# A first stage rearranged: modulation rows on four 32-column tiles, step products inside hT's blocks, constant products in waits

## The chip, the cores and the metric

One program on one core of a Trainium2 chip. The number is the device time in microseconds of one execution, and the median of several. TensorE has a granted clock with two levels here, shown as 1.00 (2.4 GHz) and 0.50 (1.2 GHz).

## What is computed

Two transformer-like blocks on 512 tokens of width 1024, all in fp32; the change touches only the first steps of the first block:

```
mod   = silu(c)     @ w_mod + b_mod              # 6 parts: sh1, sc1, g1, sh2, sc2, g2
mod_c = silu(c_ctx) @ w_mod[:, :2D] + b_mod[:2D] # sh1_c, sc1_c
hc = rmsnorm(ctx, norm1_w) * (1 + sc1_c) + sh1_c # 256 context rows
h  = rmsnorm(x, norm1_w)   * (1 + sc1) + sh1     # 512 rows
dt = softplus(h @ w_in[:, OFF_DT:OFF_CF] + dt_bias)   # 64 columns, for both h and hc
```

Behind them come the projections, the scans, a mixture of experts and a second block, which are as before.

## The kernel before

The program writes each engine's queue by hand; `Steps` objects are semaphores with named steps, where `done` marks one and `after` waits for one. Six weight buffers `slot` of 2 MB stand in SBUF, and PSUM is the tensor `ps` of eight banks of 512 columns.

The first stage is everything ahead of the loop `pe.Fori(0, GROUPS)`, whose first products are those of line 1820.

- SP loads `w_mod` in four chunks of 2 MB into slots 0 to 3, with `xcT` (x and context, transposed, 3 MB) between the second and third (lines 1213, 1214). When the rows of the last chunk are done it goes on to the loop's weights. ScalarE's queue issues `prm`, `cst` and `w_dt` (lines 1358 to 1360).
- ScalarE computes `silu_c` (both conditioning vectors, 8 blocks of 2 columns), then the squares of `xcT` for the norm (`norm1.on_act`, line 445) and the roots (448).
- TensorE waits for `silu_c` and `cst`, makes the modulation rows of chunks 0 and 1 (line 1770: weights `silu_c[:, k, :]` of two columns, moving 512 columns of the chunk, eight k for each chunk, into two partitions of PSUM), then the sums of squares with the `ones` matrix (line 431), then chunks 2 and 3. An fp32 matrix product is two records in the trace; a transpose is one.
- VectorE takes the reciprocals of the roots (465), copies the rows out of PSUM (2375), and TensorE turns them into columns with 16 transposes (1774). VectorE adds the bias, makes `mod_scale` (2378 to 2384), and scales `hT` block by block (471); ScalarE adds the shift to each block (454).
- TensorE multiplies `hT` by `w_dt` (line 1786: six groups of 128 tokens, eight k for each, weights 128x128 of `hT`, moving 64 columns of `w_dt`). The outer loop is over token groups, so only the first group's products can follow the blocks as they come.
- Then `softplus` on VectorE and ScalarE (2391 to 2397, 1372 to 1376), three small cumulative products (1791, 1795, 1797) with their exponentials (1378 to 1382), and the loop begins.

Of the kernel before, what the change touches and what calls it, by code (L numbers as in the profile page):

```python
# [10 lines left out]
ACT = mybir.ActivationFunctionType  # L11
# [3 lines left out]
P = 128  # L15
D = 1024
KD = D // P
SEQ = 512
# [3 lines left out]
ALLT = TT + CT  # L22
# [30 lines left out]
PAIR_TABLE = UNITS // 2 + 3  # L53
# [66 lines left out]
class Columns:  # L120
# [8 lines left out]
    def __getitem__(self, name):  # L129
        a, n = self.at[name]  # L130
        return slice(a, a + n)


CST = Columns([("ident", P), ("ones", P), ("le", P), ("gt", P), ("ge", P), ("lt", P),
               ("expert", NE), ("odd", NE), ("unit", TABLE), ("filled", SEQ // UNIT), ("eps", 1), ("one", 1),
               ("spot", P), ("pair", PAIR_TABLE + 1), ("token", SEQ // P)])
PRM = Columns([("c", 2 * KD), ("b_mod", 2 * N_MOD * KD), ("norm1", KD), ("norm2", KD), ("final", KD),
               ("conv", GROUPS * 8 * (CONV_K + 1)), ("ssd_norm", 2 * KD),
               ("dt_bias", 2 * N_HEADS), ("a_log", 2 * N_HEADS), ("d_skip", N_HEADS), ("b_router", NE),
# [4 lines left out]
def program(nc, io):  # L144
# [22 lines left out]
    area = Area(FREE)  # L167
    slot = [area(f"slot{i}", [P, CHUNK]) for i in range(6)]
    SLOT_BYTES = CHUNK * 4
    cst = area("cst", [P, CST.width])  # L170
    prm = area("prm", [P, PRM.width])
# [3 lines left out]
    ps = nc.alloc_psum_tensor("ps", [P, 8, 512], F32)  # L175

    ident = cst[:, CST["ident"]]
# [3 lines left out]
    def sem(name):  # L181
        return nc.alloc_semaphore(name)
# [349 lines left out]
    area = Area(STAGE)  # L532
    hT = area("hT", [P, KD, W1])
# [1 line left out]
    mod_scale = area("mod_scale", [P, KD, 2])  # L535
    AFTER_H = area.next
    xcT = area("xcT", [P, KD, W1])
    silu_c = area("silu_c", [P, KD, 2])
    square = [area(f"square{i}", [P, W1]) for i in range(2)]
    root = area("root", [P, W1])  # L540
    mod_row = area("mod_row", [2, 2 * D // 512, 512])
    w_dt = area("w_dt", [P, KD, 2 * N_HEADS])

    s_cst = sem("s_cst")
    s_prm = sem("s_prm")
    s_x = sem("s_x")
    c_silu = Steps(sem("c_silu"), ["silu"])


    MOD_CHUNKS = 2 * D // 512  # L550
    MOD_FIRST = 2 * KD
    mods_pe = Steps(sem("mods_pe"), [f"rows{c}" for c in range(MOD_CHUNKS)] + ["turned"])
    mods_dve = Steps(sem("mods_dve"), ["rows", "bias"])
    for c in range(MOD_CHUNKS):
        loads[c] += 16

# [1 line left out]
    norm1 = Norm("norm1", KD, X_PARTS, lambda i: xcT[:, i, :], lambda i: hT[:, i, :],  # L558
                 lambda i, p: mod_scale[:, i, p:p + 1], lambda i, p: mod[:, i, p:p + 1],
                 square, root, 4, 1.0 / D)  # L560
# [5 lines left out]
    area = Area(AFTER_H)  # L566
    small = area("small", [P, 5, ALLT, 2 * N_HEADS])
    AFTER_SMALL = area.next
    area = Area(AFTER_SMALL)
# [7 lines left out]
    dt_psum = ps[:, 0, 0:ALLT * 64].rearrange("p (t h) -> p t h", h=64)  # L577
# [12 lines left out]
    area = Area(FREE + 2 * SLOT_BYTES, FREE + 6 * SLOT_BYTES)  # L590
# [9 lines left out]
    area = Area(AFTER_SMALL)  # L600
# [63 lines left out]
    area = Area(AFTER_Y)  # L664
# [6 lines left out]
    area = Area(AFTER_Y)  # L671
# [3 lines left out]
    area = Area(AFTER_F)  # L675
    c_row = area("c_row", [P, D])
    dft_seq = area("dft_seq", [P, 2 * SEQ])
    area = Area(AFTER_F)
    gate_sT = [area(f"gate_sT{i}", [P, 2, SEQ]) for i in range(2)]
    area = Area(FREE + SLOT_BYTES, FREE + 2 * SLOT_BYTES)  # L680
# [3 lines left out]
    area = Area(AFTER_H, AFTER_SMALL)  # L684
# [10 lines left out]
    area = Area(AFTER_SMALL)  # L695
    f_dim = area("f_dim", [P, 4, FG, P])
    area = Area(AFTER_SMALL)
# [4 lines left out]
    area = Area(FREE + 3 * SLOT_BYTES, FREE + 4 * SLOT_BYTES)  # L702
    odd_f = area("odd_f", [P, FG, HT])
    s_two = [area(f"s_two{i}", [P, KD2, P]) for i in range(4)]
    area = Area(FREE + 3 * SLOT_BYTES, FREE + 4 * SLOT_BYTES)
    s_one = [area(f"s_one{i}", [P, KD2, P]) for i in range(4)]
    f2T = at("f2T", [P, KD, SEQ], FREE + 5 * SLOT_BYTES)
    area = Area(AFTER_Y + KD * SEQ * 4)
    f2_t = [area(f"f2_t{i}", [P, KD2, HT]) for i in range(3)]
    area = Area(FREE + 2 * SLOT_BYTES)  # L710
# [79 lines left out]
    area = Area(STAGE, AFTER_H)  # L790
# [15 lines left out]
    area = Area(AFTER_H, AFTER_SMALL + KD * SEQ * 4)  # L806
# [29 lines left out]
    area = Area(AFTER_X1)  # L836
# [7 lines left out]
    spot = area("spot", [P, TT * TOPK])  # L844
# [24 lines left out]
    area = Area(STAGE, AFTER_H)  # L869
# [3 lines left out]
    area = Area(AFTER_ROUTE, AFTER_SMALL + KD * SEQ * 4)  # L873
    b_row = area("b_row", [P, 2, 512])
    area = Area(AFTER_X1)
# [4 lines left out]
    area = Area(AFTER_X1 + 36 * 1024)  # L880
# [31 lines left out]
    area = Area(FREE + 3 * SLOT_BYTES, FREE + 6 * SLOT_BYTES)  # L912
    picked_rows = [area(f"picked_rows{i}", [P, TOPK, D]) for i in range(2)]
    moe_tok = [area(f"moe_tok{i}", [P, D]) for i in range(2)]
    area = Area(AFTER_X1)
# [14 lines left out]
    area = Area(STAGE)  # L930
# [17 lines left out]
    area = Area(AFTER_FINAL)  # L948
# [13 lines left out]
    area = Area(AFTER_V)  # L962
# [83 lines left out]
    area = Area(AFTER_V)  # L1046
# [23 lines left out]
    area = Area(AFTER_V)  # L1070
# [12 lines left out]
    area = Area(STAGE + 2 * KD * T2 * 4 + (KD + 1) * T2 * 4, AFTER_V)  # L1083
# [3 lines left out]
    area = Area(FREE + 3 * SLOT_BYTES, FREE + 5 * SLOT_BYTES)  # L1087
    rnn_w = [area(f"rnn_w{i}", [P, KD, 2, P]) for i in range(4)]
    area = Area(FREE + 5 * SLOT_BYTES, FREE + 6 * SLOT_BYTES)
# [49 lines left out]
    area = Area(AFTER_V)  # L1139
# [68 lines left out]
    @block.sync  # L1208
    def _(sp):

        for c in range(MOD_CHUNKS):
            if c == MOD_CHUNKS // 2:
                sp.dma_start(xcT[:], io["xcT"]).then_inc(s_x, 16)
            sp.dma_start(slot[c][:], io["w_mod"][c]).then_inc(w_loaded[c], 16)


# [139 lines left out]
    def _(act):  # L1356
# [3 lines left out]
        act.dma_start(w_dt[:], io["w_dt"]).then_inc(s_wdt, 16)  # L1360

        act.wait_ge(s_prm, 16)
        c_silu.done(act.activation(silu_c[:].rearrange("p k c -> p (k c)"), prm[:, PRM["c"]], ACT.Silu), "silu")
        act.wait_ge(s_cst, 16)
        act.wait_ge(s_x, 16)
        norm1.on_act(act)
# [164 lines left out]
        for i in range(2 * TT):  # L1531
            t = i // 2
# [227 lines left out]

    @block.tensor
    def _(pe):
        c_silu.all(pe)
        pe.wait_ge(s_cst, 16)
        for c in range(MOD_CHUNKS):
            if c == MOD_CHUNKS // 2:
                norm1.on_pe(pe)
            pe.wait_ge(w_loaded[c], 16)
            for k in range(KD):
                last = pe.matmul(ps[0:2, c, :], silu_c[:, k, :], slot[c][:, k * 512:(k + 1) * 512], start=(k == 0), stop=(k == KD - 1))  # L1770
            mods_pe.done(last, f"rows{c}")
        mods_dve.after(pe, "rows")
        for m in range(MOD_FIRST):
            last = pe.transpose(ps[:, 6, 2 * m:2 * m + 2], mod_row[:, m // 4, (m % 4) * P:(m % 4 + 1) * P], cst[0:2, 0:2])
        mods_pe.done(last, "turned")

        norm1_ready = norm1.ready_on(pe)  # L1780
        pe.wait_ge(s_wdt, 16)
        for t in range(ALLT):
            for k in range(KD):
                if t == 0:
                    norm1_ready(k)
                last = pe.matmul(dt_psum[:, t, :], hT[:, k, t * P:(t + 1) * P], w_dt[:, k, :], start=(k == 0), stop=(k == KD - 1))
        dt_pe.done(last, "raw")
        dt_dve.after(pe, "da")
        for d, (end, into) in enumerate([("gt", "le"), ("lt", "ge")]):
            heads = slice(d * N_HEADS, (d + 1) * N_HEADS)  # L1790
# [579 lines left out]
    def _(dve):  # L2370
        dve.wait_ge(s_x, 16)
        norm1.invert(dve)

        mods_pe.after(dve, f"rows{MOD_CHUNKS - 1}")
        mods_dve.done(dve.tensor_copy(mod_row[:], ps[0:2, 0:MOD_CHUNKS, :]), "rows")
        dve.wait_ge(s_prm, 16)
        mods_pe.after(dve, "turned")
        mods_dve.done(dve.tensor_tensor(mod[:, 0:MOD_FIRST, :].rearrange("p m c -> p (m c)"), ps[:, 6, 0:2 * MOD_FIRST],
# [693 lines left out]

    @block.gpsimd
    def _(pool):
        pool.memset(zero[:], 0.0).then_inc(s_zero, 1)


# [135 lines left out]
def shape_constants():  # L3213

    f = np.float32
    cst = np.zeros((P, CST.width), f)
    a, b = np.arange(P)[:, None], np.arange(P)[None, :]
    cst[:, CST["ident"]] = a == b
    cst[:, CST["ones"]] = 1
    cst[:, CST["le"]] = a <= b  # L3220
    cst[:, CST["gt"]] = a > b
    cst[:, CST["ge"]] = a >= b
    cst[:, CST["lt"]] = a < b
    cst[:, CST["expert"]] = np.arange(NE)
    cst[:, CST["odd"]] = 2 * np.arange(NE) + 1
    cst[:, CST["unit"]] = np.arange(TABLE) - 1
    cst[:, CST["filled"]] = np.concatenate([[-1], UNIT * np.arange(1, SEQ // UNIT)])
    cst[:, CST["eps"]] = EPS
    cst[:, CST["one"]] = 1
    cst[:, CST["spot"]] = b - P  # L3230
    cst[:, CST["pair"]] = P * np.arange(PAIR_TABLE + 1)
    cst[:, CST["token"]] = P * np.arange(SEQ // P)[None, :] + a
    t = np.arange(SEQ)
    angle = 2 * np.pi * ((t[:, None] * t[None, :]) % SEQ) / SEQ
    half = SEQ // 2
    cos, sin = np.cos(angle[0:half, 0:half + 1]) / 256.0, np.sin(angle[0:half, 1:half]) / 256.0
    dft_seq = np.concatenate([v.reshape(2, P, -1).transpose(1, 0, 2).reshape(P, -1) for v in (cos, sin)], 1)
    angle = 2 * np.pi * ((a * b) % P) / P
    alternate = np.broadcast_to(np.cos(np.pi * np.arange(half + 1)) / 256.0, (P, half + 1))
    dft_dim = np.concatenate([np.cos(angle), np.sin(angle), alternate], 1)  # L3240

    pairs = P // 4
    inv = np.exp(-np.log(f(ROPE_THETA)) * np.arange(pairs, dtype=f) / f(pairs)).astype(f)
    row = np.concatenate([np.zeros(N_META), np.repeat(np.arange(SEQ // GRID_W), GRID_W)]).astype(f)
    col = np.concatenate([np.zeros(N_META), np.tile(np.arange(GRID_W), SEQ // GRID_W)]).astype(f)
    angle = np.concatenate([inv[:, None] * row, inv[:, None] * row, inv[:, None] * col, inv[:, None] * col], 0)
    rope = np.concatenate([np.cos(angle), np.sin(angle)], 1)

    turn = np.zeros((P, P), f)
    for base in (0, 2 * pairs):  # L3250
        for i in range(pairs):
            turn[base + pairs + i, base + i] = -1
            turn[base + i, base + pairs + i] = 1
    return {"cst": cst, "dft_seq": np.ascontiguousarray(dft_seq).astype(f), "dft_dim": dft_dim.astype(f),
            "rope": np.concatenate([rope, turn], 1).astype(f)}
# [110 lines left out]
```

## Time and profile before

| | |
|---|---|
| median of 3 runs | 3529.82 us (3526.6 to 3531.34) |
| the profiled execution | 3524.86 us, span 3522.8 us |
| busy in the span | TensorE 93%, VectorE 39%, ScalarE 20%, GpSimd 11% |
| mean granted clock | 0.967 |

PE is TensorE's products, PEld its weight loads, DVE VectorE, ACT ScalarE, POOL GpSimd, SP the load queue; a trailing q is an engine's sequencer. Of the last chain of waits TensorE holds 77%. Of two times in a row of groups the first is the time in which at least one of the group ran, the second the mean length of one; products overlap, so the first over the count is the pace. Times in the timeline and the chain are from the start of the span.

### The profile page before, as it was taken

Reading aid. Unit: us, or ns where it says so; the run is one execution under the profiler, and the core shown is the slowest. Engines: PE = TensorE matmul, PEld = TensorE weight load, DVE = VectorE, ACT = ScalarE, POOL = GpSimd, SP = SyncE. Lnnn points to the kernel's source line nnn. Section 1 sums busy time; section 2 is a strip of 40 time slices with the busy share of each in tenths; the row PEclk is TensorE's granted clock in tenths of the full one; section 3 lists DMA queues with packets and bytes.
Section 4 is the critical chain, followed back from the end, with each engine's and each line's share of the span. In section 5 each row is a group of like instructions: output and inputs, shape, how many; then the busy total and the mean of one; then the engine's idle time right before and its main releaser. Section 6 shows DMA issues by size and latency. Waiting matters only on the chain.

```text
span 3522.8 us, 41282 instructions
## 1 busy us (share of the span) xinstructions
PE 3265.9 (93%) x14038; PEld 1918.0 (54%) x14039; DVE 1385.7 (39%) x2197; ACT 719.0 (20%) x1273; POOL 388.0 (11%) x303
## 2 busy tenths in 40 slices
PE   7989999999999799999999999995888899999999
PEld 3545555555587633333333333332666788878887
DVE  1354545464445522221122211223555577443342
ACT  2212121211021211111111111110322255311100
POOL 0121212232100100000000000001010155100000
PEclk8999999999999799999999999996899999999999
DMA  4030312133512379999999997793210021212211
GB/s 192 1 115 23 113 34 91 55 123 141 203 71 99 132 290 393 390 380 381 390 393 378 386 393 292 293 366 133 106 48 0 12 81 69 84 56 88 72 72 51
DMA packets 185071, 615.60 MB, mean 175 GB/s; under 512 B 18176, under 2 KB 55168, under 8 KB 174240
## 3 DMA queue, kind: packets, MB, share of 16 engines
q1 hardware_dynamic: 161168, 552.66, 41.2%
q0 software_dynamic: 10944, 39.85, 3.2%
q10 hardware_dynamic: 12880, 22.01, 1.7%
q8 instruction: 53, 0.87, 0.1%
q14 instruction: 26, 0.21, 0.0%
HBM read 578.01 MB, written 36.44 MB: 174 GB/s over the span
## 4 chain that ended last, share of the span: by engine, by line
PE 77%; DVE 6%; issue 6%; DMA 6%; POOL 2%; ACT 2%; SPq 1%; DVEq 0%; ACTq 0%; POOLq 0%
PE ps L311 22%; PE ps L2125 15%; PE ps L2101 10%; PE ps L1820 6%; PE ps L260 6%; DMA slot<-in_w_exp 5%; PE ps L1889 3%; PE ps L2310 2%; PE ps L1899 1%; PE ps L2266 1%; PE ps L1865 1%; PE ps L431 1%; PE ps L1770 1%; PE ps L2282 1%; DVE row_max L2875 1%
## 5 line engine op out<-in xcount | busy, mean ns | idle before, releaser
L2125 PE MATMUL ps<-slot,xT_blk 128*64 128x512 f32 x3200 | 735.1, 599 | 35.9 <-DMA slot<-in_w_exp 28.8
L2125 PEld LDWEIGHTS ps<-slot,xT_blk 128*64 128x64 f32 x3200 | 218.0, 137 | 474.2 <-issue 382.0
L2101 PE MATMUL ps<-slot,aT 128*64 128x512 f32 x1632 | 362.8, 597 | 0.9 <-ACT aT L1585 0.9
L1820 PE MATMUL ps<-hT,slot 128*128 128x512 f32 (+1 forms) x896 | 309.6, 504 | 1.1 <-ACT small L1382 1.1
L2101 PEld LDWEIGHTS ps<-slot,aT 128*64 128x64 f32 x1632 | 117.5, 137 | 237.9 <-issue 237.9
L1820 PEld LDWEIGHTS ps<-hT,slot 128*128 128x128 f32 x896 | 169.4, 192 | 130.9 <-issue 121.9
L2797 DVE TENSOR_TENSOR gate<-ps,b_row 128x512 f32<-128x512 f32 x50 | 34.6, 691 | 511.9 <-PE ps L2125 511.9
L2429 DVE SCALAR_TENSOR_TENSOR conv<-ps,g_conv,conv 128x510 f32<-128x510 f32 (+1 forms) x224 | 133.3, 631 | 198.8 <-ACT conv L1395 195.4
L2793 DVE MEMSET b_there<- 128x1 f32 x50 | 3.0, 59 | 390.3 <-DMA b_few<-in_b_gu 379.4
L311 PE MATMUL ps<-in_t,in_s 128*128 128x264 f32 x528 | 124.7, 386 | 0.5 <-issue 0.5
L1889 PE MATMUL ps<-hT,slot 128*128 128x512 f32 x256 | 115.2, 592 | 0.0
L3155 POOL TENSOR_TENSOR token_there<-cst 128x1 f32<-128x1 f32 x25 | 4.8, 193 | 956.2 <-PE ps L2092 956.2
L311 PEld LDWEIGHTS ps<-in_t,in_s 128*128 128x128 f32 x528 | 100.2, 190 | 18.0 <-issue 0.9
L260 PE MATMUL ps<-gate_yT,slot 128*128 128x512 f32 x256 | 110.0, 592 | 0.0
L1560 ACT ACTIVATE y_row<-ps 128x512 f32<-128x512 f32 x51 | 30.4, 597 | 385.2 <-PE ps L2101 385.2
L260 PE MATMUL ps<-xnT,slot 128*128 128x264 f32 x384 | 94.0, 408 | 11.8 <-DVE attnT L1032 6.7
L311 PE MATMUL ps<-xnT,in_w 128*128 128x264 f32 x352 | 87.7, 394 | 7.5 <-issue 7.5
L3081 POOL TENSOR_TENSOR x_end<-x_tok,g_small 128x3072 f32<-128x3072 f32 x8 | 46.6, 5826 | 417.4 <-ACT x_tok L1414 417.4
L260 PEld LDWEIGHTS ps<-xnT,slot 128*128 128x128 f32 x384 | 77.7, 203 | 27.3 <-DVE attnT L1032 7.1
L1580 ACT ACTIVATE sig<-gate 128x512 f32<-128x512 f32 x50 | 31.5, 631 | 293.8 <-DVE gate L2799 293.8
L3094 POOL TENSOR_TENSOR da_upto<-cst,g_small 128x1024 f32<-128x1024 f32 x32 | 68.2, 2132 | 134.3 <-PE ps L1865 134.3
L260 PEld LDWEIGHTS ps<-gate_yT,slot 128*128 128x128 f32 x256 | 48.6, 190 | 60.8 <-issue 59.6
(475 smaller groups left out, 4858.7 us busy)
## 6 DMA issues: line engine op xcount, KB each, us to landing
slot<-in_w_exp SPq DMA_DIRECT2D x768, 512.0 KB, 8.6
in_w<-in_w_ffn SPq DMA_DIRECT2D x22, 1024.0 KB, 4.8
expert_rows<-zero SPq DMA_DIRECT2D x4, 4608.0 KB, 22.4
slot<-in_w_xbc SPq DMA_DIRECT2D x8, 2048.0 KB, 10.2
w_modT<-in_w_modT POOLq DMA_DIRECT2D x32, 512.0 KB, 3.8
rnn_w<-in_w_rnn SPq DMA_DIRECT2D x16, 1024.0 KB, 4.8
expert_rows<-y_row ACTq DMA_DIRECT2D x102, 128.0 KB, 5.6
out_w<-in_w_ffn_out SPq DMA_DIRECT2D x8, 1408.0 KB, 9.1
```

The costliest lines, as they stand in the source:

```text
L260: last = pe.matmul(self.bank(j, part), self.layout(slot[s], m, k), self.rhs(k, part), start=(k == 0), stop=(k == self.k - 1))
L311: last = pe.matmul(out, lhs[:, k, :], rhs(k), start=(start and k == 0), stop=(k == self.kh - 1), skip_group_check=not start)
L431: last = pe.matmul(ps[:, self.bank + p, 0:n], ones, self.square[i % 2][:, c0:c0 + n], start=(i == 0), stop=(i == self.k - 1))
L1770: last = pe.matmul(ps[0:2, c, :], silu_c[:, k, :], slot[c][:, k * 512:(k + 1) * 512], start=(k == 0), stop=(k == KD - 1))
L1820: last = pe.matmul(ps[:, 2 * (m % 2) + part, 0:n], w[:, (k * 4 + m % 4) * P:(k * 4 + m % 4 + 1) * P], hT[:, k, c0:c0 + n], start=(k == 0), ...
L1889: last = pe.matmul(ps[:, 3, :], slot[1][:, (k * 4 + j // 2) * P:(k * 4 + j // 2 + 1) * P], hT[:, k, 0:SEQ], start=(k == 0), stop=(k == KD ...
L2101: last = pe.matmul(ps[h * UNIT:(h + 1) * UNIT, 6, :], aT[:, t, d * UNIT:(d + 1) * UNIT], slot[4 + d][:, t * D + h * 512:t * D + (h + 1) * ...
L2125: last = pe.matmul(ps[h * UNIT:(h + 1) * UNIT, 2 * s + t, :], xT_blk[:, k, s * UNIT:(s + 1) * UNIT], slot[i // 4][:, at:at + 512], start=( ...
L2310: last = pe.matmul(ps[:, 2 * (j % 4) + p, 0:H2], slot[j // 4][:, (k * 4 + j % 4) * P:(k * 4 + j % 4 + 1) * P], attnT[:, k, p * H2:(p + 1) ...
L2429: last = dve.scalar_tensor_tensor(out=conv[:, c0 + lo:c0 + hi], in0=ps[:, 2 * (m % 2) + part, lo + off:hi + off], scalar=g_conv[:, m, k:k ...
L3081: ssd_pool.done(pool.tensor_tensor(x_end[:].rearrange("p t (h c) -> p t h c", c=HD), x_tok[:].rearrange("p t (h c) -> p t h c", c=HD), per ...
L3094: ssd_pool.done(pool.tensor_tensor(da_upto[:], cst[:, CST["ge" if d else "le"]].unsqueeze(1).broadcast_to([P, HPG, P]), per_head(DA, t, d, ...
```

## The change

- SP issues `xcT` first and then the four chunks of `w_mod`.
- `silu_c` becomes 32 columns wide for each k, cleared on GpSimd (semaphore `s_row_tile`), with the two vectors in its first two columns. The product of block k goes to the partitions of quadrant k % 4 in PSUM, so each of four 32-column tiles sums two blocks. Turning a row into a column is now an ordinary product of the full 128 rows of `mod_row` with a new constant `context` of two columns, which also adds the four quadrants.
- The sums of squares come ahead of all four chunks on TensorE.
- VectorE copies the rows of each chunk by itself, all 128 partitions, and the turning waits chunk by chunk.
- The step products have k outside and the token groups inside, in one PSUM bank.
- `keep_warm(n, bank)` issues n products of constants, 256 columns each, into a bank that nothing reads: 6 ahead of chunk 3, 3 ahead of the last four turning products, 6 behind them, 10 behind the step products.

```diff
@@ -131,9 +131,10 @@
         return slice(a, a + n)
 
 
+ROW_TILE = 32
 CST = Columns([("ident", P), ("ones", P), ("le", P), ("gt", P), ("ge", P), ("lt", P),
                ("expert", NE), ("odd", NE), ("unit", TABLE), ("filled", SEQ // UNIT), ("eps", 1), ("one", 1),
-               ("spot", P), ("pair", PAIR_TABLE + 1), ("token", SEQ // P)])
+               ("spot", P), ("pair", PAIR_TABLE + 1), ("token", SEQ // P), ("context", 2)])
 PRM = Columns([("c", 2 * KD), ("b_mod", 2 * N_MOD * KD), ("norm1", KD), ("norm2", KD), ("final", KD),
                ("conv", GROUPS * 8 * (CONV_K + 1)), ("ssd_norm", 2 * KD),
                ("dt_bias", 2 * N_HEADS), ("a_log", 2 * N_HEADS), ("d_skip", N_HEADS), ("b_router", NE),
@@ -535,13 +536,14 @@
     mod_scale = area("mod_scale", [P, KD, 2])
     AFTER_H = area.next
     xcT = area("xcT", [P, KD, W1])
-    silu_c = area("silu_c", [P, KD, 2])
+    silu_c = area("silu_c", [P, KD, ROW_TILE])
     square = [area(f"square{i}", [P, W1]) for i in range(2)]
     root = area("root", [P, W1])
-    mod_row = area("mod_row", [2, 2 * D // 512, 512])
+    mod_row = area("mod_row", [P, 2 * D // 512, 512])
     w_dt = area("w_dt", [P, KD, 2 * N_HEADS])
 
     s_cst = sem("s_cst")
+    s_row_tile = sem("s_row_tile")
     s_prm = sem("s_prm")
     s_x = sem("s_x")
     c_silu = Steps(sem("c_silu"), ["silu"])
@@ -550,7 +552,7 @@
     MOD_CHUNKS = 2 * D // 512
     MOD_FIRST = 2 * KD
     mods_pe = Steps(sem("mods_pe"), [f"rows{c}" for c in range(MOD_CHUNKS)] + ["turned"])
-    mods_dve = Steps(sem("mods_dve"), ["rows", "bias"])
+    mods_dve = Steps(sem("mods_dve"), [f"rows{c}" for c in range(MOD_CHUNKS)] + ["bias"])
     for c in range(MOD_CHUNKS):
         loads[c] += 16
 
@@ -1208,9 +1210,8 @@
     @block.sync
     def _(sp):
 
+        sp.dma_start(xcT[:], io["xcT"]).then_inc(s_x, 16)
         for c in range(MOD_CHUNKS):
-            if c == MOD_CHUNKS // 2:
-                sp.dma_start(xcT[:], io["xcT"]).then_inc(s_x, 16)
             sp.dma_start(slot[c][:], io["w_mod"][c]).then_inc(w_loaded[c], 16)
 
 
@@ -1360,7 +1361,8 @@
         act.dma_start(w_dt[:], io["w_dt"]).then_inc(s_wdt, 16)
 
         act.wait_ge(s_prm, 16)
-        c_silu.done(act.activation(silu_c[:].rearrange("p k c -> p (k c)"), prm[:, PRM["c"]], ACT.Silu), "silu")
+        act.wait_ge(s_row_tile, 1)
+        c_silu.done(act.activation(silu_c[:, :, 0:2], prm[:, PRM["c"]].rearrange("p (k c) -> p k c", c=2), ACT.Silu), "silu")
         act.wait_ge(s_cst, 16)
         act.wait_ge(s_x, 16)
         norm1.on_act(act)
@@ -1760,31 +1762,41 @@
 
     @block.tensor
     def _(pe):
+        pe.wait_ge(s_cst, 16)
+
+        def keep_warm(n, bank):
+            for _ in range(n):
+                pe.matmul(ps[:, bank, 0:256], ident, cst[:, 0:256], start=True, stop=True)
+
+        norm1.on_pe(pe)
         c_silu.all(pe)
-        pe.wait_ge(s_cst, 16)
         for c in range(MOD_CHUNKS):
-            if c == MOD_CHUNKS // 2:
-                norm1.on_pe(pe)
+            if c == MOD_CHUNKS - 1:
+                keep_warm(6, 7)
             pe.wait_ge(w_loaded[c], 16)
             for k in range(KD):
-                last = pe.matmul(ps[0:2, c, :], silu_c[:, k, :], slot[c][:, k * 512:(k + 1) * 512], start=(k == 0), stop=(k == KD - 1))
+                q = k % (P // ROW_TILE)
+                last = pe.matmul(ps[q * ROW_TILE:(q + 1) * ROW_TILE, c, :], silu_c[:, k, :], slot[c][:, k * 512:(k + 1) * 512],
+                                 start=(k < P // ROW_TILE), stop=(k >= KD - P // ROW_TILE))
             mods_pe.done(last, f"rows{c}")
-        mods_dve.after(pe, "rows")
         for m in range(MOD_FIRST):
-            last = pe.transpose(ps[:, 6, 2 * m:2 * m + 2], mod_row[:, m // 4, (m % 4) * P:(m % 4 + 1) * P], cst[0:2, 0:2])
+            if m == MOD_FIRST - 4:
+                keep_warm(3, 7)
+            mods_dve.after(pe, f"rows{m // 4}")
+            last = pe.matmul(ps[:, 6, 2 * m:2 * m + 2], mod_row[:, m // 4, (m % 4) * P:(m % 4 + 1) * P], cst[:, CST["context"]],
+                             start=True, stop=True)
         mods_pe.done(last, "turned")
-
-
-
+        keep_warm(6, 7)
 
         norm1_ready = norm1.ready_on(pe)
         pe.wait_ge(s_wdt, 16)
-        for t in range(ALLT):
-            for k in range(KD):
-                if t == 0:
-                    norm1_ready(k)
-                last = pe.matmul(dt_psum[:, t, :], hT[:, k, t * P:(t + 1) * P], w_dt[:, k, :], start=(k == 0), stop=(k == KD - 1))
+        for k in range(KD):
+            norm1_ready(k)
+            for t in range(ALLT):
+                last = pe.matmul(dt_psum[:, t, :], hT[:, k, t * P:(t + 1) * P], w_dt[:, k, :], start=(k == 0 and t == 0), stop=(k == KD - 1),
+                                 skip_group_check=True)
         dt_pe.done(last, "raw")
+        keep_warm(10, 7)
         dt_dve.after(pe, "da")
         for d, (end, into) in enumerate([("gt", "le"), ("lt", "ge")]):
             heads = slice(d * N_HEADS, (d + 1) * N_HEADS)
@@ -2371,8 +2383,9 @@
         dve.wait_ge(s_x, 16)
         norm1.invert(dve)
 
-        mods_pe.after(dve, f"rows{MOD_CHUNKS - 1}")
-        mods_dve.done(dve.tensor_copy(mod_row[:], ps[0:2, 0:MOD_CHUNKS, :]), "rows")
+        for c in range(MOD_CHUNKS):
+            mods_pe.after(dve, f"rows{c}")
+            mods_dve.done(dve.tensor_copy(mod_row[:, c, :], ps[:, c, :]), f"rows{c}")
         dve.wait_ge(s_prm, 16)
         mods_pe.after(dve, "turned")
         mods_dve.done(dve.tensor_tensor(mod[:, 0:MOD_FIRST, :].rearrange("p m c -> p (m c)"), ps[:, 6, 0:2 * MOD_FIRST],
@@ -3072,6 +3085,7 @@
 
     @block.gpsimd
     def _(pool):
+        pool.memset(silu_c[:], 0.0).then_inc(s_row_tile, 1)
         pool.memset(zero[:], 0.0).then_inc(s_zero, 1)
 
 
@@ -3228,6 +3242,7 @@
     cst[:, CST["eps"]] = EPS
     cst[:, CST["one"]] = 1
     cst[:, CST["spot"]] = b - P
+    cst[:, CST["context"]] = a % ROW_TILE == np.arange(2)
     cst[:, CST["pair"]] = P * np.arange(PAIR_TABLE + 1)
     cst[:, CST["token"]] = P * np.arange(SEQ // P)[None, :] + a
     t = np.arange(SEQ)
```

## Rows read from the trace of the kernel before

**Rows 1.** The page: clock by slice (in tenths), and one kind of DMA issue.

```profile
PEclk8999999999999799999999999996899999999999
...
slot<-in_w_xbc SPq DMA_DIRECT2D x8, 2048.0 KB, 10.2
```

**Rows 2.** The chain of waits, 0 to 140 us: start us, us, what.

```profile
1.18 14.98 DMA cst<-in_cst
...
16.25 15.19 PE ps L1770 x32
31.44 10.52 PE ps L431 x32
41.96 13.84 PE ps L1770 x32
...
55.82 2.29 DVE mod_row L2375
...
58.16 1.16 PE ps L1774 x16
...
60.05 1.16 DVE hT L471 x2
...
61.24 8.54 ACT hT L454 x16
...
69.82 17.77 PE ps L1786 x82
...
87.61 0.57 DVE dt_raw L2391
...
92.44 1.65 PE ps L1791 x4
...
97.73 22.41 PE ps L1820 x64
...
120.81 10.32 PE ps L1820 x32
```

**Rows 3.** Windows: stretch, its length, busy of each engine, granted clock, DMA.

```profile
70.00:80.00 10.00, 10.00 (x48) 10.00 (x48) 0.00 (x0) 1.32 (x2) 0.00 (x0) 0.50 0.00 0
...
1190.30:1192.40 2.10, 2.10 (x11) 2.10 (x12) 0.00 (x0) 0.00 (x0) 0.00 (x0) 0.50 0.96 289
```

**Rows 4.** DMA queues, 10 to 12.5 us: packets, MB, share.

```profile
q1 hardware_dynamic: 52, 0.85, 79.4%
q10 hardware_dynamic: 53, 0.23, 22.1%
```

**Rows 5.** DMA queues, 17.5 to 20 us, while xcT moves.

```profile
q1 hardware_dynamic: 42, 1.03, 95.8%
```

**Rows 6.** DMA, 0 to 10 us.

```profile
DMA packets 343, 3.08 MB, mean 308 GB/s; under 512 B 32, under 2 KB 32, under 8 KB 181
```

**Rows 7.** DMA, 30 to 35 us.

```profile
DMA packets 76, 0.98 MB, mean 197 GB/s; under 512 B 16, under 2 KB 16, under 8 KB 16
```

**Rows 8.** Groups of 0 to 130 us: count | busy us, mean ns | idle before.

```profile
L445 ACT ACTIVATE square<-xcT 128x768 f32<-128x768 f32 x8 | 6.6, 840 | 23.5 <-DMA xcT<-in_xcT 13.9 <-PE ps L431 9.6
...
L465 DVE RECIPROCAL root<-root 128x512 f32<-128x512 f32 (+1 forms) x2 | 5.0, 2524 | 42.7 <-ACT root L448 42.7
```

**Rows 9.** Groups by shape, whole span.

```profile
L2125 PE MATMUL ps<-slot,xT_blk 128*64 128x512 f32 x3200 | 735.1, 599 | 35.9 <-DMA slot<-in_w_exp 28.8 <-DVEq L96 7.0
...
L2125 PEld LDWEIGHTS ps<-slot,xT_blk 128*64 128x64 f32 x3200 | 218.0, 137 | 474.2 <-issue 382.0 <-DMA slot<-in_w_exp 92.1
...
L1899 PE MATMUL ps<-x_dt,decay 128*128 128x64 f32 x512 | 60.6, 272 | 0.0
...
L2867 DVE COPY probsT<-ps 88x528 f32<-88x528 f32 x48 | 33.8, 704 | 5.1 <-PE ps L2230 4.7
```

**Rows 10.** Timeline of TensorE, 203 to 214 us: start us, us, what.

```profile
205.67 1.90 PE L1899 MATMUL ps<-x_dt,decay 128*128 128x64 f32 x16
207.40 1.08 PE L1904 MATMUL ps<-state,cT 128*128 128x512 f32 x2
```

## The prediction

> **What bounds the kernel now.** I read the page first: TensorE is busy 93% of the span, so nearly everything is its queue, and the granted clock is full except in the first slice and a few later ones [rows 1]. The diff touches only the code ahead of the group loop, whose first matmul (line 1820) starts at 97.73 us. Every later stage waits for the one before it, not for a fixed time, so what the change is worth is how much earlier that matmul starts, and at which clock. So I read the chain of waits from 0 to that point [rows 2]. It is one thread: the constants land (16.16); TensorE runs the modulation rows of chunks 0 and 1, then the sums of squares, then chunks 2 and 3, without a gap (16.25 to 55.80); VectorE copies the rows (2.29), sixteen transposes (1.16), three small VectorE steps, the blocks of hT at 1.07 us each (8.54 for the eight on ScalarE), and only then 82 of the 96 step-product records at 0.217 each (17.77). A chain of VectorE and ScalarE steps (4.83 us, 87.61 to 92.44) and three small product pairs follow.
>
> The windows show the clock [rows 3]: 0.50, the 1.2 GHz level, while the step products run back to back. The late rise costs 1.77 us in the group loop too: its first 64 records take 22.41 where a later 32 take 10.32 [rows 2].
>
> **Start of the work.** xcT moves from third to first on SP's queue, the four chunks behind it. The queues alternate packet for packet (52 against 53 in 2.5 us) [rows 4], so what lies beside cst matters. xcT's packets are 1.03 MB / 42 = 24.5 KB [rows 5], so its 3.15 MB are 128 of them, as many as prm has; 3.08 MB have moved by 10 us [rows 6]; xcT with most of prm is 3.43 MB, so it lands near 10.8 at 0.43 MB/us. Chunk 0's packets (16 KB) then run beside cst's: 2.6 MB more and a rest, so cst lands near 17.6, 1.4 us later than now. The bounds: 12.3 (all of xcT, prm and cst, nothing else, at the same rate) and 19. The last byte stays at about 32.7, since the sum of bytes is the same (0.98 MB after 30 us at that rate) [rows 7].
>
> The first square follows (0.84) [rows 8], so TensorE starts at 18.5 with the sums. They take 10.52 at full clock, and the first stretch at half clock costs 1.35 (the first 32 records took 15.19, the later 32 took 13.84) [rows 2]: to 30.3. The new memset on GpSimd is before 1 us and the silu waits for prm in any case; both lie under cst's wait. The reciprocals (5.0 together) follow the root, which is no longer than a square, and run on VectorE to about 36, beside the chunks [rows 8].
>
> **Modulation rows.** Today 64 records of 512 columns, 0.43 each, 27.5 us [rows 2]. Now each k goes to one of four 32-column tiles. The trace has no four-tile product. The nearest is the expert product, 128x512 on two 64-column tiles: 3200 records in 735.1 us, 0.230 each, though one lasts 599 [rows 9]; two run in the time of one. If four do, a chunk is four records deep, 1.7 us, and four chunks 6.8. The bounds are 0.107 a record (6.8) and 0.43 (27.5); I take 6.8, since the two-tile rows show no loss beyond their waits. The Trainium skill, "TensorE: Matmul & The Clock Gate", section "Measured speedup vs the span model", gives 2.38 for three column tiles and 3.07 for four row tiles. By 3.07 the chunks would be 27.5/3.07 = 9.0, 2.2 us later. "TensorEngine Tiling (Array Packing)", section "Key Properties", says a change of tiling mode drains the engine, which speaks against interleaving full-width products with the tiles; no row here prices it alone, and one drain bounded by the part of a record that overlaps (599 less 430 ns) would make six switches 1.0 us.
>
> Chunks 0 to 2 have landed (chunk 2 at 32.7 less 2.1 MB at 0.43, 27.8) and run to 35.4. Six constant products of 256 columns, twelve records of 0.213 (half of a 512-column record), are 2.6 us to 38.0. They hide nothing here: chunk 3 has landed at 32.7. That is a cost of the edit, kept in the sum. Chunk 3 to 39.7. The copies are now 128x512 each on VectorE; the nearest row is an 88x528 copy out of PSUM at 704 ns [rows 9], so 0.7; three start when the reciprocals end and finish by 38.1, before they are needed; only the fourth follows chunk 3, and it is hidden by the twelve columns that need chunks 0 to 2.
>
> **Turning the rows.** Sixteen transposes become sixteen ordinary products with 128x128 weights and two moving columns, two records each. The nearest record with such weights and few columns is L1899's: sixteen from 205.67 to 207.40, at least 0.108, and 0.118 over all 512 [rows 9, 10]; I take 0.112. So 24 records 2.7, three constant products 1.3, eight records 0.9: to 44.6. Today's bound from below, 1.16/16, is for two rows of weights. The three VectorE steps take 0.8 as now, and hT starts at 45.4 against 60.05: 14.6 us earlier. The six constant products behind (2.6, to 47.2) lie under hT's first block, ready 2.3 after hT's start (now 61.24 and an eighth of 8.54, 62.3), at 47.7.
>
> **Step products.** With k outside, each block lets twelve records go instead of two. At 0.112 twelve need 1.35 where a block comes every 1.07, so TensorE sets the pace: 96 records, 10.8 us, to 58.5. At half clock 96 times 0.217 would be 20.8 [rows 2]. From hT's start that is 13.1 against 27.5 now (60.05 to 87.59): another 14.4. Both bounds of the record are kept below.
>
> **The rest.** Ten constant products (20 records, 4.3) fit under the unchanged 4.83 chain at full clock; without that cover they would be pure delay, 8.5 at half. The three small pairs and ScalarE's exponentials take 5.29 (92.44 to 97.73) at half clock [rows 2]. The first pair is 1.65; three such, overlapping a little, are about 4.2 of it, and that part halves: 2.1 less (bounds 0 and 2.6). The group loop then starts warm: 1.77 less.
>
> Sum: 14.6 + 14.4 + 2.1 + 1.8 = 32.9. One deduction: around the sixteen turning products TensorE has 3.6 us with hardly any moving columns. Short records do lose the clock: in a later stage TensorE ran 32-column and then 1-column records, and between 1190.30 and 1192.40 the clock was 0.50 with the engine busy all the while [rows 3]. If that happens here, the next constant products and eight records run at half, about 2.8 us. I take it as an even chance, 1.5 us. That leaves 31 us: 3524.9 (the profiled execution's own time, span 3522.8) less 31 is 3494; the median of the runs lies 5 us above that execution, so **3499**. A difference under 0.2% (7 us) is no difference for this kernel.
>
> **Rivals.**
> 1. *The clock falls inside the step products.* They are 64 columns on 128x128 weights, and at half clock 17.8 us of them never raised it [rows 2, 3]. For the clock to hold speaks that L1899's sixteen records of the same shape run at 0.108, full clock, though only ahead of wide ones [rows 10]. If it falls about 4 us in, some 31 records pass at 0.112 and 65 at 0.217: 17.6, +6.8; the ten constant products then begin at half and take about 5.9 against 4.83: +1.1. 3507.
> 2. *Only two tiles run together.* 64 records at 0.213 are 13.6, +6.8: 3506.
> 3. *The tiles run one after another.* +20.6: 3520, and the gain is that of the reordered step products and the warmer clock alone.
> 4. *Slower.* Each record on another tile waits for the one before to drain and for its own weights: 599 + 137 (the 64-column load) = 0.736 [rows 9] instead of 0.107, 64 of them 47 us, +40: 3539. It decides above about 0.7 a record; below, the rest still pays. The two-tile rows speak against it.
> 5. *No change.* Something of fixed time behind 97.73, a load or GpSimd's part, takes the gain back. Against it: the group loop's weights are asked for when chunk 3 is done, today at 55.8 with 10.2 to land [rows 1], 31 us before their use; then near 40, against a use at 67.
>
> **Chances.** Forecast 0.57 (its own range 3493 to 3504: cst's landing, 0.108 to 0.118, the clock around the turning products), rival 1 0.16, rival 2 0.12, rival 3 0.07, rival 4 0.02, rival 5 0.03, more gain than 3491 0.03. The range 3491 to 3514 takes the forecast and the first two, with sums of parts of both; it leaves out rivals 3 to 5. Faster 0.94, same 0.04, slower 0.02.
>
> **What the new profile would show.** xcT landing near 11 and cst near 17.6; the sums from 18.5; four chunks of 16 records in about 1.7 each, the records starting in fours; hT's first block near 45; L1786 in about 10.8 at clock 1.00; L1820 near 67 and its first 32 records in 10.3. The prediction fails most where two guesses stand: the tiles' rate, and the clock in the long run of 64-column products.

## The result, and the profile after

The changed kernel takes 3498.24 us (median of 4 runs, 3494.18 to 3499.5), against 3528.21 for the kernel before (median of 4 runs). The ratio is 0.9914, with a 95% interval of 0.9902 to 0.9927. That is 30.0 us less; 31 were forecast, and 3499. The profiled execution took 3497.84, with a span of 3496.0.

The chain of waits of the changed kernel, start us, us, what, for [rows 2]:

```profile
1.18 16.81 DMA cst<-in_cst
...
19.00 12.45 PE ps L432 x32
31.44 5.29 PE ps L1779 x48
36.73 2.79 PE ps L1769 x12
39.52 1.85 PE ps L1779 x16
41.37 2.77 PE ps L1786 x24
44.14 1.40 PE ps L1769 x6
45.54 0.80 PE ps L1786 x8
...
47.08 1.16 DVE hT L472 x2
...
49.53 10.92 PE ps L1796 x96
...
65.31 0.92 PE ps L1803 x4
...
68.60 20.90 PE ps L1832 x64
```

The modulation rows, two stretches of 13.8 to 15.2 us before, are now 5.29 and 1.85 (line 1779). Line 1769 is the constant products. Between hT's start and the end of the step products (line 1796) lie 13.4 us where there were 27.5. The loop's first product (line 1832, before 1820) starts at 68.60 instead of 97.73, and the chain from the last step product to the first small pair is 4.86, unchanged.

The weight loads of the chunks, from TensorE's timeline, show how four tiles run:

```profile
31.83 0.13 PEld L1779 LDWEIGHTS ps<-slot,silu_c 128*32 128x32 f32 x4 [0.30 <-issue]
32.26 0.13 PEld L1779 LDWEIGHTS ps<-slot,silu_c 128*32 128x32 f32 x4 [0.30 <-issue]
```

They come in fours, 0.43 us from one four to the next, the time that one record of 512 columns took alone. The DMA issues, with the time to landing last:

```profile
xcT<-in_xcT SPq DMA_DIRECT2D x1, 3072.0 KB, 10.8
cst<-in_cst ACTq DMA_DIRECT2D x1, 538.5 KB, 16.8
```

xcT was issued at 0.74 and lands at 11.5, cst, issued at 1.18, at 18.0.

The windows, for [rows 3], give the granted clock in the third column from the end. The first is the step products, the second a stretch of the group loop:

```profile
49.53:60.30 10.77, 10.77 (x97) 10.77 (x97) 6.11 (x12) 8.80 (x16) 0.00 (x0) 1.00 0.35 149
...
150.00:160.00 10.00, 7.03 (x10) 2.89 (x10) 7.81 (x12) 1.91 (x2) 0.00 (x0) 0.66 0.96 328
```

The second line is where part of the lead goes again. The kernel before has the same work about 30 us later, at full clock:

```profile
179.00:190.00 11.00, 6.87 (x17) 2.60 (x15) 8.71 (x13) 3.67 (x4) 0.94 (x1) 1.00 0.91 286
```

The two profiled spans differ by 26.8 us only, although the loop starts 29.1 us earlier and 1.5 us less cold (20.90 for its first 64 records against 22.41). What lies behind the loop's start took 3425.1 us in the profile before and 3427.4 in this one. The experiments measure how much that part varies by itself.

### The profile page after: what moved, and what is told of

Same layout as the page of the kernel before. It is cut to its first block, busy times and chain, and to the rows that moved or that the text cites. A ratio compares the mean times of both kernels' runs of the same rounds, so it can differ in the third digit from the quotient of the medians.

```text
span 3496.0 us, 41420 instructions
## 1 busy us (share of the span) xinstructions
PE 3252.2 (93%) x14104; PEld 1917.5 (55%) x14105; DVE 1386.7 (40%) x2200; ACT 718.9 (21%) x1273; POOL 388.5 (11%) x304
## 4 chain that ended last, share of the span: by engine, by line
PE 77%; DVE 7%; issue 6%; DMA 5%; POOL 2%; ACT 2%; SPq 1%; DVEq 0%; ACTq 0%; POOLq 0%
PE ps L312 22%; PE ps L2137 16%; PE ps L2113 10%; PE ps L1832 6%; PE ps L261 6%; DMA slot<-in_w_exp 5%; PE ps L1901 3%; PE ps L2322 2%; PE ps L1911 1%; PE ps L2278 1%; PE ps L1877 1%; PE ps L432 1%; PE ps L2294 1%; DVE row_max L2888 1%; PE ps L1916 1%
## 5 line engine op out<-in xcount | busy, mean ns | idle before, releaser
L261 PE MATMUL ps<-xnT,slot 128*128 128x264 f32 x384 | 94.1, 408 | 11.8 <-DVE attnT L1034 6.7
```

The source lines that it names most:

```text
L261: last = pe.matmul(self.bank(j, part), self.layout(slot[s], m, k), self.rhs(k, part), start=(k == 0), stop=(k == self.k - 1))
```

## The experiments

All are the changed kernel with one edit, except where the text says otherwise. The times of e1 to e8, e11 and e12 are of one run each. The same kernel took from 3490.31 to 3502.58 us in six runs (e10 below), so one such time does not settle a difference of up to 12 us. What settles it is the time on the chain inside the first stage, and the start of the loop.

### e1: no constant products

```diff
         def keep_warm(n, bank):
-            for _ in range(n):
+            for _ in range(0):
```

> All 25 constant products are left out, the rest is the changed kernel. Theory A, they hold the clock: without them hT starts about 4.2 us earlier (42.9, since 2.8 and 1.4 us of them lie ahead of it), but the clock falls while the rows are turned, the 96 step-product records run at 0.217 us (20.8 instead of 10.9), and the group loop's first product starts near 76 instead of 68.6, cold, which costs 1.8 more: 9 us longer than the changed kernel. Theory B, they are only delay and the clock holds without them: the loop starts near 64.4, 4 us shorter.

3501.49 us. The chain of e1:

```profile
38.84 3.68 PE ps L1786 x32
...
45.70 20.73 PE ps L1796 x96
...
76.24 20.90 PE ps L1832 x64
```

Theory A: hT starts 3.8 us earlier, the step products take 20.73, the loop starts at 76.24, 7.6 us late. Two things in it were wrong. The clock held while the rows were turned and fell only near 44 us, in the wait for hT's first block (0.99 from 42 to 44, 0.50 from 44 to 46). And the 1.8 us of a cold loop did not come: the clock had risen in the three small pairs just ahead of it (0.83 from 74 to 76), so the loop itself starts at full clock.

### e2 and e3: two tiles, and one

```diff
-                q = k % (P // ROW_TILE)
+                q = k % 2            # e3: k % 1
```

with the start and stop flags to match; the copies and the turning products use 64 partitions in e2 and 32 in e3.

> The modulation rows go to two 32-column tiles instead of four, and 64 partitions are copied and turned. Theory A, the pace is set by how many tiles run together: 0.213 us a record, a chunk 3.4 to 3.5 us instead of 1.76, hT starts 6.9 us later, near 54. Theory B, four tiles are already held back by something else (weight loads, reading): a chunk takes less than 3.4 us, and the start of hT moves by clearly less than 6.9.

> The modulation rows all go to one 32-column tile, and 32 partitions are copied and turned; the rest is the changed kernel. Theory A, four tiles were worth three quarters of the time: 0.430 us a record, a chunk 6.9 us, four chunks 27.5 instead of 7.1, hT starts 20.4 us later, near 67.5; total 20 us longer, so that only about 10 of the 30 us gained are left. Theory B, part of the gain of the tiles is taken by waits that would be there anyway (the reciprocals, the chunks' landing): less than 18 us longer.

3501.83 and 3522.69 us. The chain of e2, then that of e3:

```profile
32.01 10.42 PE ps L1779 x48
...
45.22 3.56 PE ps L1779 x16
...
51.77 2.86 PE ps L1769 x6
```

```profile
31.85 20.72 PE ps L1779 x48
...
55.36 6.98 PE ps L1779 x16
```

Forty-eight records take 20.72, 10.42 and 5.29 us on one, two and four tiles: 3.92 times as fast on four. Theory A holds in both. The loop starts at 77.89 and 94.08. Those are 2.4 and 4.9 us more than the tiles account for, and e2's chain shows where the first part is: the three constant products took 2.86 us, not 1.40. The clock fell while the rows were turned, as it did in e3, where the last eight turning records (1.79 against 0.80) and the six constant products behind them (5.22 against 2.79) ran at half as well.

### e4: token groups outside again

```diff
-        for k in range(KD):
-            norm1_ready(k)
-            for t in range(ALLT):
+        for t in range(ALLT):
+            for k in range(KD):
+                if t == 0:
+                    norm1_ready(k)
...
```

> The step products have the token groups outside again, as before, the rest is the changed kernel. While the blocks of hT come, only two records go for each. Theory A, the clock falls in that thin stretch: the last 82 records run at 0.217 us, the step products end near 74.6 instead of 60.45, and the loop starts near 84, 15 to 17 us later than in the changed kernel. Theory B, the clock holds: they end near 66, and the loop starts 5.5 us later.

3509.42 us. The chain, and the clock in the windows of e4:

```profile
59.11 17.75 PE ps L1797 x82
...
85.25 20.90 PE ps L1832 x64
```

```profile
50.00:59.00 9.00, 5.32 (x20) 3.68 (x19) 7.91 (x16) 8.47 (x16) 0.00 (x0) 0.77 0.43 186
59.00:77.00 18.00, 17.89 (x83) 17.89 (x84) 0.10 (x1) 1.60 (x3) 0.00 (x0) 0.50 0.00 1
```

Theory A: the clock is 1.00 from 48 to 54 us and falls near 55, in the thin stretch while the blocks come, the remaining 82 records go at 0.216 each, and the loop starts 16.65 us later. So the constant products alone do not save the clock of the step products: with the old order of the loops it falls behind them, in the thin stretch. Of the 16.65 us, 2.3 are a later hT, because the clock fell at the turning too, and was up again by 48.

### e5 to e7: the constant products one group at a time

```diff
-            if c == MOD_CHUNKS - 1:
-                keep_warm(6, 7)              # e5, ahead of chunk 3
...
         mods_pe.done(last, "turned")
-        keep_warm(6, 7)                      # e6, behind the turning products
...
         dt_pe.done(last, "raw")
-        keep_warm(10, 7)                     # e7, behind the step products
```

> The six constant products ahead of chunk 3 are left out, the rest is the changed kernel. Theory A, they are pure delay, since chunk 3 has landed by then: everything behind starts 2.8 us earlier, hT near 44.3 and the loop near 65.8, at full clock all the way. Theory B, they carry the clock over the turning products: without them it falls there, the turning and the constant products behind it run at half, and at least 2 of the 2.8 us are given back (hT near 46.5 or later).

> The six constant products behind the turning products are left out, the rest is the changed kernel. hT and the first step product start where they did (47.1, 49.5). Theory A, these six decide the clock of the step products: it falls in the 3.2 us without work, the 96 records take up to 20.8 us instead of 10.9, and the loop starts up to 11 us later. Theory B, the clock is kept by what is ahead and by the step products themselves: 10.9 us again, loop near 68.6.

> The ten constant products behind the step products are left out, the rest is the changed kernel. Theory A, the clock falls in the 4.8 us that TensorE then waits: the three small pairs and their exponentials take 5.3 instead of 3.3 us (loop near 70.6), and the first 64 records of the loop take 22.4 to 22.7 instead of 20.9, so 3.5 us in all. Theory B, the wait is too short for the clock to fall, and nothing moves.

3496.62, 3510.54 and 3496.34 us. The chain of e5:

```profile
42.31 2.77 PE ps L1769 x6
45.08 1.04 PE ps L1784 x8
...
46.86 1.16 DVE hT L472 x2
```

From the end of the sums to hT are 14.4 us, against 15.6 in the changed kernel: of the 2.8 us that the six cost, 1.3 are won and the rest goes in half-clock turning (2.77 and 1.04 against 1.40 and 0.80). That is between the two theories. The fall occurs in other runs with the six in place too, so one run does not tell whether the six hold it off. The chain of e6:

```profile
49.04 20.63 PE ps L1795 x96
...
78.79 20.90 PE ps L1831 x64
```

```profile
46.00:49.00 3.00, 0.00 (x0) 0.00 (x0) 2.90 (x8) 1.22 (x3) 0.00 (x0) 1.00 1.02 437
```

Theory A: without the six behind the turning products TensorE stands still from 45.9 to 49.0. The clock is 1.00 to the end of that wait and falls within 0.1 us of the first step product. The step products then run at half, and the loop starts 10.2 us late. The chain of e7:

```profile
69.11 1.65 PE ps L1802 x4
...
74.31 20.90 PE ps L1831 x64
```

From the first small pair to the loop are 5.20 us, against 3.29: the clock did fall in the wait. But it was up again in time for the loop, whose first 64 records take 20.90. So the ten are worth 1.9 us here, not 3.5.

### e8 and e9: cst first

```diff
-        act.dma_start(prm[:], io["prm"]).then_inc(s_prm, 16)
         act.dma_start(cst[:], io["cst"]).then_inc(s_cst, 16)
+        act.dma_start(prm[:], io["prm"]).then_inc(s_prm, 16)
...
+        act.wait_ge(s_zero, 1)                                    # e9 alone
+        act.activation(root[:, 0:1], zero[:, 0:1], ACT.Silu)      # e9 alone
         act.wait_ge(s_cst, 16)
         act.wait_ge(s_x, 16)
+        norm1.ready = lambda at, i: silu(at) if i == 5 else None  # the silu, moved
         norm1.on_act(act)
```

The silu and its two waits stand in a function `silu(at)` here (not shown), which is called behind the fifth square.

> The changed kernel with cst ahead of prm on ScalarE's queue, and the silu behind the fifth square. By the alternation of packets cst's 128 packets then run beside xcT's 128, and both have landed by 12.3 us, prm near 17.8; TensorE starts the sums near 13.2 and ends them near 25.5. Chunk 2 lands near 27.8 and chunk 3 near 32.7, so now loads hold the rows: chunk 3 is done near 35, 6 us earlier than in the changed kernel, the six constant products lie in that wait, hT starts near 41 and the loop near 62.5. Theory B, the queues do not alternate so and cst still waits for xcT's bytes and more: the sums start after 15, and less than 4 us are gained.

3493.02 us. The chain of e8:

```profile
0.74 11.24 DMA xcT<-in_xcT
...
12.05 1.28 ACT L446
...
14.34 5.91 PE ps L432 x12
...
21.13 1.28 ACT L1366
...
23.42 4.14 PE ps L432 x12
```

xcT and cst have landed by 12.1, as the alternation of packets gives it (12.3); Theory B had the sums start after 15, and they start at 14.3 although a table load comes first. But the silu had stood first and had loaded the activation table inside the transfers. Moved, it leaves two loads of 1.28 us on the chain (the lines of ScalarE without a tile), and hT starts at 43.20. The loop starts at 64.72, 3.9 us earlier than in the changed kernel.

> The kernel of e8 with a silu of one column right after GpSimd's memset, so that the activation table is loaded during the transfers. Theory A, the two table loads (1.28 us each) in e8's chain are what it lost: the first square goes at 12.0 instead of 13.35 and the 1.9 us gap in the sums closes to nothing, so the sums end near 25 instead of 27.6, chunk 2 (landed near 27.8) then holds the rows, and chunk 3 is done near 36 to 37: hT starts 1 to 2 us earlier than in e8 and 4 to 6 earlier than in the changed kernel. Over the whole kernel 3492, against 3498. Theory B, the group loop takes back what is gained ahead of it: no difference from the changed kernel within 0.1%.

> The changed kernel as it is, for a comparison on the same chip: 3498, with the start of the loop between 68 and 72 as the clock falls or not around the turning products, and everything behind that start between 3420 and 3430 us long.

e9 takes 3489.98 us (5 runs, 3488.64 to 3494.62), ratio to the kernel before 0.9903, interval 0.989 to 0.9916. e10, the changed kernel beside it, takes 3494.79 (6 runs, 3490.31 to 3502.58), ratio 0.9916, interval 0.9902 to 0.993. The chain of e9:

```profile
2.82 31.29 DMA slot<-in_w_mod
34.15 1.92 PE ps L1783 x16
...
41.79 1.16 DVE hT L472 x2
...
63.34 20.90 PE ps L1836 x64
```

Theory A: now a transfer, the last chunk (landed at 34.1, where the prediction had 32.7), is what the rows wait for, and hT starts at 41.79. Chunk 2 held nothing: the sums end at 25.9, and the rows of the first three chunks follow without a wait. The loop starts at 63.34, 5.3 us earlier than in the profile after. The medians differ by 4.8 us, which fits, but the intervals overlap. That the stage is shorter is shown, that the kernel is faster is not. The chain of e10 shows the changed kernel in an execution where the clock fell at the turning:

```profile
44.87 2.77 PE ps L1769 x6
47.63 1.50 PE ps L1786 x8
49.13 5.24 PE ps L1769 x12
54.37 10.68 PE ps L1796 x96
...
73.21 20.90 PE ps L1832 x64
```

The clock fell at 43.9 us, while the rows were turned, and rose at 54.1, in the last of the six constant products behind them. The loop starts at 73.21, outside the 68 to 72 that I had given. The whole is 3494.56 us all the same, less than the profiled execution above.

### e11: xcT between the chunks

```diff
-        sp.dma_start(xcT[:], io["xcT"]).then_inc(s_x, 16)
         for c in range(MOD_CHUNKS):
+            if c == MOD_CHUNKS // 2:
+                sp.dma_start(xcT[:], io["xcT"]).then_inc(s_x, 16)
```

> xcT goes back between the second and third chunk on SP's queue, the rest is the changed kernel. Theory A, the sums, which now stand first on TensorE, wait for it: xcT lands at 24 as before, the sums run from 25 to 37, hT starts near 53 and the loop near 74.6, 6 us later; cst lands at 16.2 again. Theory B, the alternation of queues gives it earlier, and less than 3 us are lost.

3505.53 us. The chain of e11:

```profile
1.64 22.50 DMA xcT<-in_xcT
...
25.21 13.15 PE ps L432 x32
```

Theory A: xcT lands at 24.1 and the sums start 6.2 us later. The loop starts at 77.20, 8.6 later; 0.7 of the rest is a longer cold start of the sums (13.15 against 12.45), and the clock fell at the turning here too.

### e12: the step products twice

```diff
+        for k in range(KD):
+            for t in range(ALLT):
+                last = pe.matmul(ps[:, 5, t * 64:(t + 1) * 64], hT[:, k, t * P:(t + 1) * P], w_dt[:, k, :], ...)
         dt_pe.done(last, "raw")
```

> The 96 step-product records are issued a second time into another bank right behind the first, the results of the second not used; the rest is the changed kernel. Theory A, a long run of such records holds the clock once it is up: both hundreds take 10.7 to 10.9 us, and the loop starts 10.7 us later, near 79.3. Theory B, the constant products ahead only delay the fall: the second set runs at 0.217 us a record, up to 20.8 us, and the loop starts up to 21 us later.

3504.67 us. The chain, and one window of e12:

```profile
49.49 10.90 PE ps L1796 x96
60.40 10.73 PE ps L1800 x96
```

```profile
60.00:70.00 10.00, 10.00 (x92) 10.00 (x91) 0.00 (x0) 0.00 (x0) 0.00 (x0) 1.00 0.01 2
```

Theory A: full clock for 21.6 us of these records, the loop at 79.29.

## Why the prediction was right, step by step

**Start.** xcT at 11.5 (forecast 10.8) and cst at 18.0 (17.6). The sums started at 19.0, not 18.5, and took 12.45, not 11.8: the first stretch at half clock was longer. The granted clock is on record only from its first change on (22.8 us here; the windows show 1.00 ahead of it), so the pace has to tell it. Three weight loads of the sums take 1.19 us early on and 0.62 later:

```profile
20.83 1.19 PEld L432 LDWEIGHTS ps<-square,cst 128*128 128x128 f32 x3 [0.52 <-issue]
24.40 0.62 PEld L432 LDWEIGHTS ps<-square,cst 128*128 128x128 f32 x3 [0.24 <-issue]
```

The cost above 10.52 was 1.9 us, where the prediction had taken 1.35 from the kernel before. Over the twelve profiles with this order and no gap in it the sums took 11.95 (e6) to 13.63 us (e7), so that term has a spread of its own, which the prediction left out. Why it varies stays open. At 31.4 the chain was 1.1 us late.

**Modulation rows.** 1.76 us a chunk against 1.7; rivals 2 to 4 are out, and e2 and e3 show their price, 6.8 and 20.6 us of rows as worked out. The 3.07 that the Trainium skill, "TensorE: Matmul & The Clock Gate", section "Measured speedup vs the span model", gives for four row tiles would have made the four chunks 9.0 us; they took 7.1, and e3's pace over this one's is 3.92, so the measurement decides. The switches between tiled and full-width products cost little (the stage has four, not six): the twelve constant records took 2.79 instead of 2.56, and the chunk behind them 1.85 instead of 1.76, at most 0.3 us together. Most of it is no cost of a switch: in the timeline the twelve behind the turning, with no tiles beside them, take as long (2.84 against 2.86). The six constant products ahead of chunk 3 stood in the chain for 2.8 us, as the prediction had it.

**Turning.** 0.115 us a record for the first 24 (2.77), against 0.112. hT starts at 47.08, 13.0 us earlier; forecast 14.6. The 13.0 come out of the two chains: the start is 2.75 later (19.00 against 16.25), sums, rows and constant products are 17.18 shorter (22.37 against 39.55), the copy no longer stands between rows and turning (2.36), and from there to hT it is 3.82 longer (5.71 against 1.89). The deduction of 1.5 us for a fall of the clock was not met in this execution, but it was the right kind of term. The three constant products took 1.40 us where the clock held and 2.3 or more where it fell; of the twelve profiles that have them (the changed kernel and e2 to e12), five held it and seven did not. Its size was wrong: 2.8 us were given, and e10 started its step products 4.8 us after the profile after, its sums only 0.3 later. The missing part is that the six products behind ran at half too (5.24 against 2.79) and then stood in the way of hT's first blocks.

**Step products.** 10.92 us, forecast 10.8; from hT's start to their end 14.2 us less, forecast 14.4. Rival 1, the clock lost inside them, did not occur, and in e12 it did not occur in twice the length. Nothing on record gave the 4 us that it allowed before the fall. The cover ahead of them decides: in all ten profiles with the new order and the six constant products ahead the 96 records took 10.7 to 10.9 us, also in the six where the clock had fallen at the turning, and in the two without the six (e1, e6) 20.7 and 20.6.

**The rest.** 2.0 for the small pairs (forecast 2.1) and 1.5 for the loop's start (1.8).

The four measured terms, 12.97, 14.16, 2.00 and 1.51, sum to 30.6 us; the forecast's four sum to 32.9. That the forecast of 31 was met so closely is in part luck: it had 1.5 us taken off for a fall of the clock that this execution did not have, and its four terms came out 2.3 us short, 1.6 of them ahead of hT (the start, the sums, the rows, the turning). The 3499 has a second such pair: for the profiled execution the prediction had 3494 and it took 3497.84, but the 5 us that were added for the median were not there (3498.24).

The profiled spans differ by 26.8, the medians by 30.0, and in the later comparison by 29.6 (3524.41 to 3494.79). Behind the loop's start, span less start, the 14 profiles took between 3419.5 us (e10) and 3429.9 (e6), with the same 13,820 product records. The changed kernel has both 3427.4 and 3419.5 there, and the earliest start (e9, 63.34) and the latest (before, 97.73) have 3423.4 and 3425.1. So rival 5, something that takes the gain back, is not at work; the 26.8 of the one pair of profiles lie inside the spread of that part. The clock goes with it: added up from the clock records, TensorE was at the 1.2 GHz level behind the loop's start for 189 us in the two shortest (e7, e10), 218 in the longest (e6), 194 in the profile before and 212 in the one after. It does not explain all of it (e3 has 195 us and 3426.8), and why it falls more often in one execution than in another stays open.

## What to carry to other kernels

Products whose weights have few columns gain nearly the full factor from column tiles, as these did: 3.9 for four. A stretch of short or absent work on TensorE can be paid twice, once as itself and once as the clock of what follows. So constant products pay where they stand right ahead of work that did not raise the clock by itself (10.2 us for 2.8 us of products in e6). Where the next real work is ready they delay it, and whether they give anything back was not settled (e5: 1.3 of 2.8 us won without them, in one run). Where two queues alternate packet for packet, a small constant waits for the packets beside its own, large as they are, so the order inside the small queue counts as well: cst landed at 12.1 us instead of 18.0 (e8).

## What the runs showed of the hardware

- The same stream of records (128x128 weights, 64 moving columns, back to back) kept the clock that it began with: 17.8 us of it at 0.50 did not raise it in the kernel before, nor 20.7 in e1, 17.8 in e4 and 20.6 in e6, and 21.6 us at 1.00 did not lose it in e12. (In e6 the clock fell within the first 0.1 us of the stream, behind 3.2 us without work.) So the same 96 records took 10.9 us or 20.6.
- The turning products (128x128 weights, 2 moving columns) and the three constant products among them lost the clock in seven of twelve profiles, with TensorE busy all the while. It rose again in the constant products or in the last eight turning records (at 54.1 us in e10, near 48 in e4).
- Four 32-column tiles ran side by side: 48 fp32 records of 512 moving columns took 5.29 us on four, 10.42 on two and 20.72 on one.
- Silu and the squares share an activation table: with a silu first (e9, table loaded at 2.1 us) there is no load until the roots, and with the square first there are two of 1.28 us (e8).
